# Two dense chunks of the value table in one transfer, in two places instead of four slots

## What is computed

```python
# h: (256, 2048); u, v: (16384, 2048); per token 8 heads x 16 chosen experts
eid, gate = choose(h @ wq, keys)
act = gelu(einsum('thkd,td->thk', u[eid], h))
ff = einsum('thk,thkd->td', gate * act, v[eid])
out = layernorm(ALPHA * h + ff)
```

## Time and profile before

| | us |
|---|---|
| median of three runs | 2970.9 |
| the three runs | 2967.61, 2971.24, 2970.9 |
| the profiled execution | 2968.88 |
| its span | 2967.1 |
| value stage, first plain product to last weighing | 2466.2 to about 2947.5 |
| busy in the span: TensorE, VectorE, ScalarE, GpSimd | 2323.2, 2035.6, 1129.5, 818.3 |
| plain products of the value stage, line 1155, 1024 instructions | 298.0 |
| weighings, line 2279, 254 | 293.2 |

### The profile page before, as it was taken

How to read it: one execution, slowest core, us unless ns; L and a number is a source line. 1 busy time by engine, 2 the same in 40 slices (tenths; PEclk the granted TensorE clock), 3 DMA queues, 4 the chain that set the end, 5 groups by cost and what they waited for, 6 DMA issues and landing times.

```text
span 2967.1 us, 28922 instructions
## 1 busy us (share of the span) xinstructions
PE 2323.2 (78%) x10371; PEld 1832.5 (62%) x10371; DVE 2035.6 (69%) x2513; ACT 1129.5 (38%) x1263; POOL 818.3 (28%) x646
## 2 busy tenths in 40 slices
PE   8999999999999999899999990000022249998997
PEld 7888888888888888688888770000011136555654
DVE  5456555554544555745665678999899888887888
ACT  5444344444444554444344442121222244222222
POOL 1000000000000000000000017888787875545553
PEclk9999999999999999999999995555555569999998
DMA  8666556666666546465566569999999977999997
GB/s 281 208 186 193 168 178 191 183 193 190 183 189 184 156 140 207 146 183 177 163 185 227 162 209 395 420 420 418 415 406 400 421 287 291 408 407 390 408 408 301
DMA packets 165303, 792.12 MB, mean 267 GB/s; under 512 B 20188, under 2 KB 20240, under 8 KB 131248
## 3 DMA queue, kind: packets, MB, share of 16 engines
q1 hardware_dynamic: 105344, 390.12, 41.1%
q0 software_dynamic: 59824, 400.23, 33.3%
HBM read 788.17 MB, written 2.10 MB: 266 GB/s over the span
## 4 chain that ended last, share of the span: by engine, by line
PE 57%; DVE 19%; DMA 13%; issue 6%; POOL 3%; ACT 1%; POOLq 0%; DVEq 0%; ACTq 0%
PE banks L749 52%; DMA v_rows<-in_peer_v_rest,eid 11%; DVE ring L2205 9%; DVE banks L2279 3%; DMA ring<-in_peer_u,eid 2%; POOL ring L674 2%; PE banks L781 1%; PE banks L1124 1%; POOL v_rows L716 1%; DVE onehots L2184 1%; DVE v_split L2290 1%; PE banks L761 1%; DVE w_split L1565 0%; DVE cand L2108 0%; PE banks L829 0%
## 5 line engine op out<-in xcount | busy, mean ns | idle before, releaser
L749 PE MATMUL banks<-w_split,xT 128*128 128x512 f32 x7008 | 1611.8, 391 | 8.5 <-DVE xT L1612 5.3
L749 PEld LDWEIGHTS banks<-w_split,xT 128*128 128x128 f32 x7008 | 1314.3, 188 | 282.5 <-DVE xT L1612 6.9
L1565 DVE TENSOR_TENSOR w_split<-w_raw,w_split 128x1024 fp32r<-128x1024 f32 x592 | 722.3, 1225 | 730.6 <-ACT w_split L1187 729.5
L1187 ACT ACTIVATE w_split<-w_raw 128x1024 fp32r<-128x1024 f32 x592 | 626.2, 1059 | 911.6 <-PE banks L749 875.4
L2205 DVE CUSTOM_DVE_ANT_0 ring<-ring,banks 128x2048 f32<-128x2048 f32 x194 | 438.5, 2285 | 46.3 <-DMA ring<-in_peer_u,eid 42.4
L2279 DVE SCALAR_TENSOR_TENSOR banks<-v_rows,wgt,banks 128x896 f32<-128x896 f32 x254 | 293.2, 1154 | 67.6 <-DMA v_rows<-in_peer_v_rest,eid 66.4
L674 POOL DMA_INDIRECT ring<-in_peer_u,eid x256 | 244.8, 956 | 258.4 <-DVE eid L2137 157.8
L716 POOL DMA_INDIRECT v_rows<-in_peer_v_rest,eid x256 | 245.3, 958 | 233.6 <-DVE banks L2279 202.0
L1155 PE MATMUL banks<-v_raw,wT 128*128 128x512 f32 (+1 forms) x1024 | 298.0, 434 | 0.7 <-ACT wT L1475 0.7
L609 POOL DMA_DIRECT2D row_a<-in_final_g x1 | 0.5, 534 | 1067.3 <-DVE ao L1827 1067.3
L1124 PE MATMUL banks<-onehots 128*128 128x128 f32 x512 | 103.0, 367 | 243.7 <-DVE onehots L2184 232.4
(11 more groups left out here) (321 smaller groups left out, 1320.9 us busy)
## 6 DMA issues: line engine op xcount, KB each, us to landing
w_raw<-in_a_w_in SPq DMA_DIRECT2D x192, 512.0 KB, 3.5
v_raw<-in_peer_v_dense SPq DMA_DIRECT2D x128, 576.0 KB, 8.0
w_raw<-in_b_w_in SPq DMA_DIRECT2D x128, 512.0 KB, 3.5
w_raw<-in_w_in SPq DMA_DIRECT2D x112, 512.0 KB, 3.6
w_raw<-in_a_w_out SPq DMA_DIRECT2D x64, 512.0 KB, 4.5
w_raw<-in_b_w_out SPq DMA_DIRECT2D x32, 512.0 KB, 4.5
w_raw<-in_w_out SPq DMA_DIRECT2D x32, 512.0 KB, 4.4
w_raw<-in_peer_wq SPq DMA_DIRECT2D x32, 512.0 KB, 3.7
```

The source lines that it names most:

```text
L749: last = mm(ps[half][:, 2 * t + n, :], xt[:, xp, kk, tok], w_split[:, s, wp, n * BANK:(n + 1) * BANK], start=(k == 0 and xp == 0 and wp == ...
L1187: fn(w_split[:, k % SPLIT_SLOTS, 0, :], w_raw[:, k % RAW_SLOTS, :], ACT.Copy).then_inc(hi_done, 1)
L1565: v.tensor_tensor(w_split[:, s, 1, :], w_raw[:, k % RAW_SLOTS, :], w_split[:, s, 0, :].bitcast(F32), ALU.subtract).then_inc(split_done, 1)
```

## The change

The dense part of `v` is laid out anew by the host: chunks 2p and 2p+1 form pair p, and for each of 128 partitions the 4608 bytes of the first chunk's expert and the 4608 bytes of the second's follow each other. One load brings a pair: 9216 contiguous bytes per partition, 1152 KB. Four slots of one chunk become two places of two chunks, with a semaphore for each place; the place of pair p is loaded again for pair p+2 when both of its chunks are multiplied. Place 0 lies where slots 0 and 1 were, together with one of the two buffers of rounded parts (`v_split`); place 1 lies in the region of the one-hots and is first filled after the last scatter. What the engines compute, and in which order, stays.

```diff
--- before.py
+++ after.py
@@ -70,6 +70,8 @@
 V_PLAIN = tuple((lo, min(BANK, V_DENSE - lo)) for lo in range(V_SPLIT, V_DENSE, BANK))
 V_BANKS = 1 + len(V_PLAIN)
 V_CHUNKS = 4
+V_PAIR = 2
+V_PAIRS = V_CHUNKS // V_PAIR
 V_SLOTS = 6
 V_EARLY = 4
 SCATTER = 4
@@ -384,9 +386,9 @@
         early_raw = packer(RAW, 16 * KB)
         early_rows = packer(ROWS, LISTS)
         late = packer(SCR + 32 * KB, 16 * KB + 512)
-        v_split = [late(f"v_split{n}", [P, 2, V_SPLIT], F32R) for n in range(2)]
-        v_raw = ([early_raw(f"v_raw{n}", [P, V_DENSE]) for n in range(V_CHUNKS - 1)]
-                 + [late(f"v_raw{V_CHUNKS - 1}", [P, V_DENSE])])
+        v_split = [put(f"v_split{n}", [P, 2, V_SPLIT], F32R) for n, put in enumerate((early_raw, late))]
+        v_pair = [put(f"v_pair{n}", [P, V_PAIR, V_DENSE]) for n, put in enumerate((early_raw, late))]
+        v_raw = [v_pair[n // V_PAIR][:, n % V_PAIR, :] for n in range(V_CHUNKS)]
         v_rows = ([early_rows(f"v_rows{n}", [P, V_GATHERED]) for n in range(V_EARLY)]
                   + [late(f"v_rows{V_EARLY}", [P, V_GATHERED]),
                      sb(f"v_rows{V_EARLY + 1}", [P, V_GATHERED], F32, ROWS + 24 * KB - V_ROW)])
@@ -489,7 +491,7 @@
         weighed_by_act = sem("weighed_by_act")
         scattered = sem("scattered")
         w_stored = sem("w_stored")
-        v_raw_landed = [sem(f"v_raw_landed{s}") for s in range(V_CHUNKS)]
+        v_raw_landed = [sem(f"v_raw_landed{s}") for s in range(V_PAIRS)]
         v_products = sem("v_products")
         v_landed = [sem(f"v_landed{n}") for n in range(V_SLOTS)]
         v_used = sem("v_used")
@@ -576,20 +578,21 @@
             load_pairs(w_out_2[0], "mix_out", 0, 1)
             load_pairs(peer_wq_2[0], "peer_q", 0, 1)
 
-            def load_v(c, s):
-
-                if not isinstance(c, int):
-                    sp.wait_ge(v_products, c + (1 - V_CHUNKS))
-                elif s + 1 == V_CHUNKS:
+            def load_v(p, s):
+
+                if not isinstance(p, int):
+                    sp.wait_ge(v_products, p * V_PAIR + (V_PAIR - V_CHUNKS))
+                elif s + 1 == V_PAIRS:
                     sp.wait_ge(scattered, TOKENS // SCATTER + 2)
-                sp.dma_start(v_raw[s][:, :], peer_v_dense[0, bass.ds(c * N_KEYS, N_KEYS), :]).then_inc(v_raw_landed[s], 16)
+                sp.dma_start(v_pair[s][:, :, :].rearrange("p k d -> p (k d)"), peer_v_dense[bass.ds(p * P, P), :])\
+                    .then_inc(v_raw_landed[s], 16)
 
             sp.wait_ge(keys_known, TILES)
-            for s in range(V_CHUNKS):
+            for s in range(V_PAIRS):
                 load_v(s, s)
             with sp.Fori(1, N_KEYS // V_CHUNKS) as i:
-                for s in range(V_CHUNKS):
-                    load_v(i * V_CHUNKS + s, s)
+                for s in range(V_PAIRS):
+                    load_v(i * V_PAIRS + s, s)
             for n in range(2 * TILES):
                 t, b = divmod(n, 2)
                 cols_ = slice(b * COLS, (b + 1) * COLS)
@@ -1149,7 +1152,7 @@
                     return mm(v_banks[t][0], w_x[u][:, wp, 1 - t, :], v_split[u][:, vp, :],
                               start=first and wp + vp == 0, stop=last and vp == 1)
 
-                pe.wait_ge(v_raw_landed[s], 16 * (c // V_CHUNKS + 1))
+                pe.wait_ge(v_raw_landed[s // V_PAIR], 16 * (c // V_CHUNKS + 1))
                 for t in range(TILES):
                     for n, (lo, width) in enumerate(V_PLAIN):
                         mm(v_banks[t][1 + n][:, 0:width], wT[:, 1 - t, c, :], v_raw[s][:, lo:lo + width],
@@ -1527,7 +1530,7 @@
                 if c >= 2:
                     act.wait_ge(v_products, c - 1)
                 fn(w_x[u][:, 0, :, :], wT[:, :, c, :], ACT.Copy).then_inc(w_hi, 1)
-                act.wait_ge(v_raw_landed[c % V_CHUNKS], 16 * (c // V_CHUNKS + 1))
+                act.wait_ge(v_raw_landed[c % V_CHUNKS // V_PAIR], 16 * (c // V_CHUNKS + 1))
                 fn(v_split[u][:, 0, :], v_raw[c % V_CHUNKS][:, 0:V_SPLIT], ACT.Copy).then_inc(v_hi, 1)
 
             def keep_sum(t):
@@ -2346,7 +2349,8 @@
 
     nc = bacc.Bacc("TRN2", target_bir_lowering=False, num_devices=1)
     arrays, args = {}, []
-    inputs["peer_v_dense"] = inputs["peer_v_2"][:, :, :V_DENSE]
+    dense = inputs["peer_v_2"][0, :, :V_DENSE].reshape(N_KEYS // V_PAIR, V_PAIR, N_KEYS, V_DENSE)
+    inputs["peer_v_dense"] = dense.transpose(0, 2, 1, 3).reshape(-1, V_PAIR * V_DENSE)
     inputs["peer_v_rest"] = inputs["peer_v_2"][:, :, V_DENSE:]
     for name in _INS:
         a = np.ascontiguousarray(inputs[name])
```

## The result

| | before | after |
|---|---|---|
| median, us | 2971.07 (2967.61 to 2972.91, 4 runs) | 3053.72 (3038.47 to 3057.11, 4 runs) |
| after / before, 95% interval | | 1.0269 (1.025 to 1.0288) |
| span of the profiled execution, us | 2967.1 | 3052.7 |

The account below looks back on a forecast made before the run. The prediction took the transfer rate as the limit, by 0.14 us a chunk over TensorE. Its terms, -4.4 + 0.5 = -3.9 us, gave 2967.0 us against the median of 2970.9, with a range of 2958 to 2988.

Parts of the forecast that it names:

- Step 1: Value stage's dense loads: half as many pieces, four fewer per engine and chunk at 9.1 ns each, -4.4 us (0 to -12).
- Step 2: Start of the value stage: two fewer chunks loaded ahead, one load more inside the stage, +0.5 us (0 to 1.4).
- Step 3: Dense loads released and issued later, two chunks ahead in place of three; landing taken as 7.0 us, cost 0 us.
- The law of the round: A place's four chunks of time T each equal landing L plus 7.3 us: two TensorE chunks and 0.2 for semaphore and SP.
- a cover of 0.3 us: Margin of the forecast 7.0 us landing of a pair against the 7.3 us allowed at T = 3.66.
- Rival A: TensorE at each pair's first chunk: the dense load becomes the wait from a 7.5 us landing; +16 to about +20 us, chance 0.35.
- The damping: In rival A, loads land sooner once DMA engines are no longer full, cutting +46 us at a 9.0 us landing to about +20.
- Step 4: Gathers behind a pair's burst of 2.8 us, where it was 1.4: VectorE can catch up, 0 us.
- Step 5: Remaining parts (moved rounded-parts buffer, 64 loads issued by SP, ScalarE and TensorE waits): nothing on a path; slack covers ScalarE's longer wait.

Follow-up runs that it names:

- The candidate: Kernel before with 32 columns moved from the gathered to the dense part (V_GATHERED 864 in place of 896): 2959.0 us, ratio 0.9952.
- turning the order: Kernel after, with the four gathers that follow each pair held on GpSimd until that pair is multiplied: 3022.2 us, ratio 1.0166.
- the filled gap: Kernel after, with 0.85 us of products with zeros ahead of each TensorE wait for a pair but the first: 3043.8 us, ratio 1.0239.
- Two halves: Kernel after, with each pair brought by two transfers of 4608-byte pieces, TensorE and ScalarE still waiting for both: 3094.5 us, ratio 1.0391.

## Why the prediction was wrong, point by point

*What bounds the kernel.* Right: the transfer rate, 0.14 us a chunk ahead of TensorE. The candidate, which shifts 0.11 us to TensorE and relieves the transfers, agrees with the balance by its steady distance (3.64 for 3.69). Step 1, the price of a piece: right in size (9.1 ns; 10.5 measured, with smaller pieces). The estimate from the Trainium skill ("DMA: Bandwidth & Descriptors", section "Why small descriptors are slow (HBM only)"), -2 us for 4 x 120 pieces per engine, is 4 ns a piece; the measurement is above twice that, and decides. Its gain of 4.4 us needs full DMA engines, and the kernel after has them at 0.93, so it never came. Step 2, the start: not contradicted (0.5 forecast; the interval of the run is -2 to +4 us).

*Step 3 is the step that failed*: "I take 7.0 and 0 us". The law of the round, 4T = L + 7.3, was right: with T = (3013.9 - 2485.1) / 120 = 4.41 us, from the first and the last steady issue, it asks for 10.3 us of landing and delays, and the chain's landings of mostly 8 to 10 us with 0.85 us of slow clock per round (27 us over 32 rounds) come to that. The size of L was wrong, by 2 to 3 us: 7.0 forecast, 9.3 on the mean of the chain. I had built it from the first load of 2268, which was served ahead of the gathers for its 8 pieces. A pair is issued in another moment: TensorE has just finished a pair, and VectorE has been freeing slots. Around the pair issued at 2609.03, GpSimd issues gathers at 2604.67, 2605.93, 2607.92 and 2609.18. Rows for such a moment were there, the 8.0 us of the steady loads, and I explained them away as the rest of the load before. Halving the gathers (6.4 us) and turning the order (8.1 us) show whose time it is. I noted a cover of 0.3 us and should have asked what moves together with the issue.

Rival A had the mechanism, the place and the deciding point (7.5 us), but a price of 16 to 20 us. Two terms were wrong. The damping that I counted on, loads landing sooner once the DMA engines have room, didn't come: the share is 0.93 and the landings are still 9 us. And the clock wasn't in any sum. By the rival's own formula without the damping, a landing of 9.3 us gives T = (9.3 + 7.3) / 4 = 4.15, 0.46 over 3.69 and 57 us over 123 chunks; with 27 us of clock that is 84, and 83 were measured. The clock costs 27 us by the timeline; the filled gap brought 10 back net, and the run with fewer products lost all that it had saved.

*Step 4* (gathers behind a longer burst): right in its 0 us, VectorE waited 1.5 us for rows; but at a chunk of 4.4 us in place of 3.66 the gathers have time that step 4 didn't count on, so the run doesn't test it at the forecast's pace. *Step 5*: right that nothing is on the path by itself, wrong that ScalarE's slack covers its wait: VectorE waits 133.7 us for ScalarE, though behind the same landing that TensorE waits for.

What stays open: how the 9 us divide into waiting behind gathers and taking turns with them piece by piece. Two halves (10.1 for 9.3 us) and the pieces of 2304 bytes (10.9 for 8.0 us) speak for turns by piece, turning the order (8.1 us) for gathers ahead; no run separates the two.

## What to carry to other kernels

When slots are merged into larger ones, write down the round of a slot (issue, landing, use until the release) and compare it with the time the round may take, with the landing of the steady state, not of a quiet moment: the landing is made by what is issued just before. A transfer must be whole before any of it can be used, so twice the size in the same memory halves the number of places, and the next load is issued one chunk later (here two chunks ahead of its use in place of three). Where TensorE then waits, price the clock behind the gap as well.

## What the runs showed of the hardware

- In the kernel after, behind 14 of 17 waits of 2.3 to 3.5 us TensorE's next 8 plain products took 3.4 to 4.6 us in place of 2.4, with a granted clock of 0.66 in the stretch looked at; behind the other three (2.54, 2.65 and 3.29 us) they took 2.43. Behind waits of at most 1.9 us they took 2.43 too, but for two, of 1.89 and 1.92 us (4.1). So the length of the wait alone doesn't tell. With 0.85 us of products with zeros ahead of the wait, which left waits of at most 2.0 us, the clock stayed at 1.00.
- A row piece costs about 10.5 ns of a DMA engine in full stretches (2304 against 4608 bytes, the smaller ones lying apart in HBM), and more pieces of the same bytes land later: 10.9 against 8.0 us.
- Less work for TensorE made the kernel slower (3064 against 3054 us): its gaps grew from 71 to 104 us and the clock fell from 0.95 to 0.88.
- A load of 1152 KB landed in 9.1 to 9.3 us beside gathers of 3584-byte rows (medians of three runs), in 8.1 us with the gathers issued behind it, and in 6.4 us beside gathers of half the bytes.
- Rows of 4736 and 3456 bytes, which are no multiples of 256, moved no slower than those of 4608 and 3584: 412 against 408 GB/s in 2500 to 2650.
